# Two halves of the tokens set apart at every change of stage, and four tiles of each FFN with tokens as rows

## Chip, cores and metric

The kernel runs on 1 core of one Trainium2 chip. The metric is the device time of one execution in microseconds (us), as the median of the runs. Computing is in float32, each product of matrices as three products of a high and a low part.

## What is computed

The reference takes x (256 tokens x 1024), and runs three blocks of layers over it. Two belong to the first model, one to the second. Each FFN is a SwiGLU of 1024 to 2 x 2816 and back, and there are six:

```python
x = x + FFN_RESIDUAL * rmsnorm(swiglu(rmsnorm(x, g[0]), ffn_w_in[i, 0], ffn_w_out[i, 0]), g[1])
h = rmsnorm(x, g[2])
...
x = x + rmsnorm(m, g[3])
x = x + FFN_RESIDUAL * rmsnorm(swiglu(rmsnorm(x, g[4]), ffn_w_in[i, 1], ffn_w_out[i, 1]), g[5])
gate = jax.nn.sigmoid(rmsnorm(x, g[6]) @ ple_w_gate[i])
x = x + rmsnorm(gate * (p[i] @ ple_w_proj[i]), g[7])
```

Here m is differential attention in the first block, and a state space layer (S5) with a gated linear unit (glu1, glu2) in the second. The third block has no norm behind an FFN; its middle is a sliding window attention and an HGRN2 recurrence side by side (the mixers), joined through `w_out`, and its gate is the last product before the final norm.

## The kernel before, in words

**Weights.** They come in 264 units of 1 MB, in the order of use, by DMAs on the SP queue into `raw` (4 buffers of a unit). A unit is two half units of 128 x 1024. For each half unit ScalarE (ACT) rounds raw to `whi` (line 600) and VectorE (DVE) makes `wlo` = raw - whi (L1060), into one of 4 slots. `use` asks for splits up to 3 half units ahead of the one in hand (`Ahead`, which goes no further than the slots that are free). A slot is free when TensorE (PE) has counted the half unit in `s_used`; a raw buffer when both of its halves have their wlo (`weights` in `sync`).

**Two forms of a product.** An up of an FFN (`half_unit`) holds weights stationary: 8 k-tiles x 3 products, 24 matmuls of 256 columns for one half unit, all 256 tokens at once, result with features as rows. `linear` and the downs hold tokens stationary (`run`): for each token half (128 tokens) and each half unit (a k-tile), 3 x 2 matmuls of 512 columns, so 12 for both halves, result with tokens as rows in four banks of PSUM. All matmuls of both have line 1740.

**An FFN.** 22 tiles of 128 features. Each tile is two ups (gate and value) and one down. Behind an up come silu on ACT (L682), the product on DVE (L1181), its high part on ACT (L686), its low part `hlo` on DVE (L1183). Pairs of tiles alternate with the downs of the pair before; the downs of the last two tiles are one `run`, half 0 before half 1.

**A change of stage.** The result y of token half h goes through these steps (`settle`, `take_turns`):

1. ACT: squares of y, each half row (L630, L633; L627 behind a gate); DVE: y x g (L1115, L1117; L1110).
2. POOL: rstd in two instructions (L490, L497); DVE: added to X (L1137).
3. ACT: squares of X (L643); POOL: rstd.
4. DVE: norm to `xn` (L1145).
5. PE: 8 transposes (L1811); ACT: high part `xhi` (L660).
6. DVE: low part `xlo` (L1165).

`ORDER` says in which turn the two halves take a step, the same on all engines. Each engine works strictly in its program's order.

```python
ORDER = (0, 0, 0, 1, 0, 1, 1, 0, 1, 0, 1, 1)
ORDER_DEFER = (0, 0, 0, 1, 0, 1, 0, 1, 0, 1)
```

With the second (`DEFER`: ahead of v of the attention, and of the gates) half 1's step 5 stands behind the second k-tile of the next `linear`. At the gates (`ple`), `proj` runs within the change of stage, ACT copies its result (L714), then come the gate's sigmoid (L718) and the product with it (L1100), each over a whole row of 1024. While the FFNs, the attention and the mixers run, `Weave` puts one step of the other work (heads, tables, recurrence) between half units at each `fill`.

## Time and profile before

| | us |
|---|---|
| median of 3 runs | 1938.12 |
| lowest, highest | 1934.77, 1940.52 |
| the profiled execution, its own time | 1937.2 |
| its span (first to last instruction) | 1935.4 |
| TensorE busy in it | 1739.7 |
| VectorE, ScalarE, GpSimd busy | 1113.4, 887.7, 132.5 |
| mean granted TensorE clock | 0.921 |
| moved by DMA | 300.95 MB, 155 GB/s |

How to read it: the profile is of one execution. A row of the timeline gives start and length, the engine, the line of the kernel, the operation with what it writes and reads, and in brackets how long the engine stood idle before it and who released it. The length of a matmul is more than its share of the engine, since matmuls overlap: the pitch is read from a piece of the chain or from two starts. The clock is 1.00 at 2.4 GHz and 0.50 at 1.2 GHz.

### The profile page before, as it was taken

The page shows a single profiled execution, that of the slowest core. Times are in us where ns is not written, and L with a number is a line of the kernel's source. Part 1 is how long each engine was busy: PE and PEld are TensorE (multiplying, and loading weights), DVE is VectorE, ACT ScalarE, POOL GpSimd, SP SyncE. Part 2 cuts the span into 40 slices and gives each one's busy share as a digit, 9 for nine tenths or more (in the row PEclk, how much of TensorE's full clock was granted, in tenths as well). Part 3 has the DMA queues.
Part 4 walks back from the last instruction along what each step waited for, and adds up shares of the span by engine and source line. Part 5 has one row for each costly group of instructions (what it writes and reads, how often), then busy time and mean ns, then how long its engine had stood idle before and what let it go on. Part 6 is the DMA issues. An engine that isn't in the chain of part 4 may idle for free.

```text
span 1935.4 us, 27710 instructions
## 1 busy us (share of the span) xinstructions
PE 1739.7 (90%) x11666; PEld 1601.0 (83%) x11666; DVE 1113.4 (58%) x1587; ACT 887.7 (46%) x1365; POOL 132.5 (7%) x197
## 2 busy tenths in 40 slices
PE   7999897699987999978488999889998997999996
PEld 7999795699976998967468999679998886899995
DVE  5555565475555744649455555555555675655554
ACT  5444554344444536430444444544445434444443
POOL 0000000100002012840000000000000000000000
PEclk9999997799998979966588999989999998999998
DMA  7654442255544533520054555445454431445550
GB/s 282 236 195 175 176 156 80 86 201 185 194 174 144 193 119 133 184 77 1 22 195 152 180 183 187 174 155 206 176 195 148 150 108 66 173 169 176 195 189 28
DMA packets 51083, 300.95 MB, mean 155 GB/s; under 512 B 6072, under 2 KB 12688, under 8 KB 17168
## 3 DMA queue, kind: packets, MB, share of 16 engines
q1 hardware_dynamic: 50800, 298.66, 43.2%
q8 instruction: 92, 1.51, 0.3%
q0 software_dynamic: 160, 0.52, 0.1%
q14 instruction: 31, 0.25, 0.0%
HBM read 298.08 MB, written 1.09 MB: 155 GB/s over the span
## 4 chain that ended last, share of the span: by engine, by line
PE 79%; DVE 9%; ACT 7%; issue 2%; POOL 2%; DMA 0%; DVEq 0%; SPq 0%; ACTq 0%; POOLq 0%
PE PS L1740 75%; DVE wlo L1060 1%; ACT wk L643 1%; PE PS L1743 1%; ACT whi L600 1%; POOL st L497 1%; PE PS L1811 1%; DVE wk L1435 1%; DVE SC L1307 1%; DVE wk L1437 1%; DVE X L1137 1%; DVE wk L1439 1%; DVE xn L1145 1%; ACT SC L820 1%; ACT SC L855 1%
## 5 line engine op out<-in xcount | busy, mean ns | idle before, releaser
L1060 DVE TENSOR_TENSOR wlo<-raw,whi 128x1024 fp32r<-128x1024 f32 x528 | 651.2, 1238 | 418.9 <-ACT whi L600 418.1
L1740 PE MATMUL PS<-xhi,whi 128*128 128x256 f32 x2536 | 730.8, 288 | 11.5 <-DVE xlo L1165 8.5
L1740 PE MATMUL PS<-xlo,whi 128*128 128x256 f32 x2536 | 725.3, 286 | 0.0
L1740 PE MATMUL PS<-xhi,wlo 128*128 128x256 f32 x2536 | 724.7, 286 | 0.0
L600 ACT ACTIVATE whi<-raw 128x1024 fp32r<-128x1024 f32 x528 | 551.8, 1054 | 368.5 <-PE PS L1740 368.4
L1740 PEld LDWEIGHTS PS<-xhi,whi 128*128 128x128 f32 x2536 | 494.5, 195 | 20.3 <-DVE xlo L1165 10.9
L1740 PEld LDWEIGHTS PS<-xlo,whi 128*128 128x128 f32 x2536 | 494.8, 195 | 2.1
L1740 PEld LDWEIGHTS PS<-xhi,wlo 128*128 128x128 f32 x2536 | 494.2, 195 | 0.0
L1740 PE MATMUL PS<-whi,hhi 128*128 128x512 f32 x544 | 169.9, 394 | 0.2 <-issue 0.2
L1740 PE MATMUL PS<-wlo,hhi 128*128 128x512 f32 x544 | 168.8, 391 | 0.0
L1740 PE MATMUL PS<-whi,hlo 128*128 128x512 f32 x544 | 168.2, 390 | 0.0
L682 ACT ACTIVATE wk<-PS 128x256 f32<-128x256 f32 x132 | 50.5, 383 | 217.6 <-PE PS L1740 217.4
L1181 DVE TENSOR_TENSOR wk<-PS,wk 128x256 f32<-128x256 f32 x132 | 55.9, 424 | 119.4 <-ACT wk L682 119.4
L1740 PEld LDWEIGHTS PS<-wlo,hhi 128*128 128x128 f32 x544 | 102.7, 189 | 22.2
L1740 PEld LDWEIGHTS PS<-whi,hlo 128*128 128x128 f32 x544 | 102.6, 189 | 21.9
L1740 PEld LDWEIGHTS PS<-whi,hhi 128*128 128x128 f32 x544 | 98.5, 190 | 17.3 <-issue 0.6
L1740 PE MATMUL PS<-whi,xhi 128*128 128x512 f32 (+1 forms) x256 | 87.3, 414 | 21.9 <-ACT SC L714 11.8
L686 ACT ACTIVATE hhi<-wk 128x256 fp32r<-128x256 f32 x132 | 55.2, 418 | 91.8 <-DVE wk L1181 91.8
L1811 PE MATMUL PS<-idt,xn 128*128 128x128 f32 x176 | 35.9, 366 | 67.8 <-DVE xn L1145 67.8
L1183 DVE TENSOR_TENSOR hlo<-wk,hhi 128x256 fp32r<-128x256 f32 x132 | 57.3, 434 | 64.0 <-ACT hhi L686 64.0
L1811 PEld LDWEIGHTS PS<-idt,xn 128*128 128x128 f32 x176 | 28.4, 189 | 75.9 <-DVE xn L1145 60.2
L490 POOL TENSOR_SCALAR st<-st 128x1 f32<-128x1 f32 x36 | 11.7, 325 | 1151.2 <-ACT wk L633 599.8
(252 smaller groups left out, 1539.3 us busy)
## 6 DMA issues: line engine op xcount, KB each, us to landing
raw<-in_w SPq DMA_DIRECT2D x264, 1024.0 KB, 4.8
gr<-in_rows SPq DMA_DIRECT2D x23, 512.0 KB, 3.8
SC<-scratch SPq DMA_DIRECT2D x1, 2048.0 KB, 8.1
SC<-scratch SPq DMA_DIRECT2D x2, 1024.0 KB, 8.5
X<-in_x SPq DMA_DIRECT2D x2, 512.0 KB, 4.4
xn<-in_sc SPq DMA_DIRECT2D x2, 512.0 KB, 7.0
out<-xn SPq DMA_DIRECT2D x2, 512.0 KB, 2.6
SC<-in_pT SPq DMA_DIRECT2D x3, 256.0 KB, 4.2
```

Source lines behind the costliest of these rows:

```text
L497: g.tensor_tensor(r, ms, mh[:, 0:max(n, 1)], ALU.pow).then_inc(done, 1)
L600: a.activation(whi[:, u % NSPLIT, :], raw[:, u // 2 % NRAW, u % 2 * HU:u % 2 * HU + HU], ACT.Copy).then_inc(s_hi, 1)
L643: a.activation(wk[:, f], X[:, h, f], ACT.Square, scale=1 / 32, accum_out=ss[:, i:i + 1]).then_inc(s_sq, 1)
L682: a.activation(sg[:, f % 2, :], PS[:, b, 0:S], ACT.Silu).then_inc(s_silu, 1)
L686: a.activation(hhi[:, f % 4, :], hf[:, f % 2, :], ACT.Copy).then_inc(s_hhi, 1)
L820: e = a.activation(cst[r, k, :, s, 16 * i:16 * i + 16], o[k][r], ACT.Copy)
L855: e = a.activation(o[32 * j:32 * j + 32, :, :, v], p[32 * v:32 * v + 32, :, j, :], ACT.Gelu_apprx_tanh)
L1060: v.tensor_tensor(wlo[:, u % NSPLIT, :], src, hi.bitcast(f32), SUB).then_inc(s_lo, 1)
L1181: v.tensor_tensor(hf[:, f % 2, :], PS[:, 4 + f % 3, S:2 * S], sg[:, f % 2, :], MUL).then_inc(s_hm, 1)
L1183: v.tensor_tensor(hlo[:, f % 4, :], hf[:, f % 2, :], hhi[:, f % 4, :].bitcast(f32), SUB).then_inc(s_hlo, 1)
L1740: return pe.matmul(o, l, r, start=start, stop=stop)
L1811: e = pe.transpose(PS[:, tr_bank(k, h, kq), 128 * i:128 * i + 128], xn[:, h, 128 * (4 * kq + i):128 * (4 * kq + i) + 128], idt[:, :])
```

## The change

- **Slots.** `raw` has 2 buffers, not 4, and `whi` and `wlo` have 6 slots, not 4. The splits no longer look at which slots are free: each place in the programs of ACT and DVE names the half unit up to which it splits (`split`).
- **Order at a change of stage.** `settle(k, h, mid, end)` does all steps of half 0, then all of half 1. Between norm and the low part stands a split up to `mid`, behind it one up to `end`.
- **PE** begins the next product with half 0: k-tiles 0 to 5, then half 1's 0 and 1, half 0's 6 and 7, half 1's 2 to 7 (`halves`); half 1's transposes stand within (behind k-tile 4 of half 0 in an FFN and 3 in v; at a gate behind 2, with the next stage's transposes of half 0 ahead of the last part).
- **FFN.** The ups of tiles 0 to 3 (8 half units) have tokens stationary, like `linear`; silu and product are in place with tokens as rows, then 4 transposes for each half, then the high and low parts. Tiles 4 and 5 each stand alone with the downs of 0 to 3 between. The tail has four tiles (`TAIL`), not two; so has `wo`, and `w_out` and `glu2` have six.
- **Gates** read `proj` from PSUM; sigmoid, product and g are done by half rows. glu2's bias has a buffer of its own. The mixers' product `ri` comes first there, half by half, where it stood between the first pairs and the rest; `fill(4)` becomes `fill(5)`.

```diff
-NRAW = 4
-NSPLIT = 4
+NRAW = 2
+NSLOT = 6
 AHEAD = 3
+NA = 4
+NW = NF - NA
+TAIL = 4
...
 def up_at(n, f):
-    return FFN_AT[n] + (2 * f if f < 2 else 4 + 6 * (f // 2 - 1) + 2 * (f % 2))
+    return FFN_AT[n] + (8, 12)[f - NA] if f < NA + 2 else FFN_AT[n] + 16 + 6 * (f // 2 - 3) + 2 * (f % 2)
 def down_at(n, f):
-    j = f // 2
-    return FFN_AT[n] + (8 + 6 * j if j < NF // 2 - 1 else 64) + f % 2
+    if f < NA:
+        return FFN_AT[n] + 10 + 4 * (f // 2) + f % 2
+    return FFN_AT[n] + (20 + 6 * (f // 2 - 2) if f < NF - 2 else 64) + f % 2
...
-        while self.n <= min(v + AHEAD, N_HALF - 1) and (self.n < NSPLIT or self.n - NSPLIT <= self.done):
+        while self.n <= min(v, N_HALF - 1):
...
-                while at[0] <= min((v + AHEAD - 1) // 2 + NRAW, N_HALF // 2 - 1):
+                while at[0] <= min((v - 1) // 2 + NRAW, N_HALF // 2 - 1):
...
-                weights(LAST[BEFORE[k]] - 1 if k else -9)
+                weights(LAST[BEFORE[k]] + 4 if k else 3)
...
+            def settle(k, h, mid=-1, end=-1):
+                times_g(k, h)
+                add_x(k, h)
+                norm(k, h)
+                split(mid)
+                evict_lo(k, h)
+                split(end)
...
             def ffn(n):
+                u0 = FFN_AT[n]
+                split(u0 + 7)
+                for h in range(2):
+                    q.wait_ge(e_silu, 2 * n + h + 1)
+                    if h:
+                        q.wait_ge(e_tr, 2 * n + 1)
+                    v.tensor_tensor(wk[:, HI], PS[:, 5 + 2 * h, :], wk[:, LO], MUL).then_inc(e_hm, 1)
+                    split(u0 + (9, 13)[h])
+                    q.wait_ge(e_hhi, 2 * n + h + 1)
+                    t = slice(128 * h, 128 * h + 128)
+                    v.tensor_tensor(hlo[:, 0:4, t], in128(PS[:, 4 + 2 * h, :]), hhi[:, 0:4, t].bitcast(f32), SUB).then_inc(e_hlo, 1)
+                    if h == 0:
...
                 k = (3, 7, 11)[layer]
-                def rest():
-                    evict_lo(k, 1)
-                take_turns(k, steps, {3: lambda: linear(f"proj{layer}", 2, head=2, tail=0)})
-                linear(f"gate{layer}", 8, head=4, tail=2, finish=rest)
-                take_turns(k + 1, steps)
+                u = PLE_AT[layer]
+                settle(k, 0, u + 2, u + 3)
+                settle(k, 1, u + 5, u + 9)
+                for h in range(2):
+                    settle(k + 1, h, *((u + 11, u + 13), (u + 15, u + 15))[h])
...
+            def run(parts, base, last, by_half=None, between={}, order=None):
+                for h, n in order or [(h, n) for h in range(2) for n in range(len(parts))]:
+                    if by_half is not None and n == 0:
                         q.wait_ge(s_xlo, n_ev(by_half, h))
-                    for n, (u, ahi, alo, first, end) in enumerate(parts):
-                        if finish and h == 0 and n == 2:
-                            finish()
-                        hi, lo = weight(u)
-                        l_hi, l_lo = ahi[:, 128 * h:128 * h + 128], alo[:, 128 * h:128 * h + 128]
-                        for i, (l, r) in enumerate(((l_hi, hi), (l_hi, lo), (l_lo, hi))):
-                            for c in range(2):
-                                e = mm(PS[:, base + 2 * h + c, :], l, r[:, 512 * c:512 * c + 512], first and i == 0, end and i == 2)
-                        if h:
-                            e.then_inc(s_used, 1)
-                        elif last and n == len(parts) - 1:
-                            e.then_inc(s_y, 1)
...
+                            at[0, n] = lambda k=k: ready(k)
...
+            def halves(*spans):
+                return [(h, n) for h, a, b in spans for n in range(a, b)]
...
                 k = (0, 2, 4, 6, 8, 10)[n]
-                def up(f):
+                def turned_half(h):
+                    b = 4 + 2 * h
+                    q.wait_ge(e_hm, 2 * n + h + 1)
+                    for i in range(4):
+                        e = pe.transpose(PS[:, b, 128 * i:128 * i + 128], wk[:, 512 + 128 * i:640 + 128 * i], idt[:, :])
+                    e.then_inc(e_tr, 1)
+                def up(f, between=None):
                     b = 4 + f % 3
-                    if f >= 3:
-                        q.wait_ge(s_hm, NF * n + f - 2)
-                    if f == 0:
-                        q.wait_ge(s_xlo, n_ev(k, 1))
-                    half_unit(up_at(n, f), PS[:, b, 0:S])
-                    bg.fill()
-                    half_unit(up_at(n, f) + 1, PS[:, b, S:2 * S])
-                    bg.fill()
+                    if f >= NA + 3:
+                        q.wait_ge(s_hm, nth(n, f) - 2)
+                    for i in range(2):
+                        half_unit(up_at(n, f) + i, PS[:, b, S * i:S * i + S])
+                        if between and i == 0:
+                            between()
+                        bg.fill()
                 def part(f):
-                    q.wait_ge(s_hlo, NF * n + f + 1)
+                    if f < NA:
+                        q.wait_ge(e_hlo, 2 * n + 2)
+                    else:
+                        q.wait_ge(s_hlo, nth(n, f) + 1)
                     return down_at(n, f), hhi[:, f % 4, :], hlo[:, f % 4, :], f == 0, f == NF - 1
-                for j in range(NF // 2):
+                def down(f):
+                    weight(down_at(n, f))
+                    run([part(f)], 0, False)
+                    bg.fill(2)
+                def other_half():
+                    transposed(k, 1)
+                    if k in GATED:
+                        q.wait_ge(s_gated, n_gate(k, 1))
+                    if k == 2:
+                        q.wait_ge(s_yg, n_yg(k, 1))
+                        q.wait_ge(s_sq, n_sq(k, 1, 1))
+                if first:
+                    transposed(k, 0)
+                linear(f"first{n}", x_acts, 4, by_half=k, between={(0, 5 if k else 2): other_half, (1, 6): lambda: turned_half(0)},
+                       order=halves((0, 0, 6), (1, 0, 2), (0, 6, 8), (1, 2, 8)), n_fill=0)
+                for f in range(NA, NA + 2):
+                    up(f, (lambda: turned_half(1)) if f == NA else None)
+                    down(2 * (f - NA))
+                    down(2 * (f - NA) + 1)
+                for j in range(3, NF // 2):
                     up(2 * j)
                     up(2 * j + 1)
-                    for f in (2 * j - 2, 2 * j - 1) if j else ():
-                        weight(down_at(n, f))
-                        run([part(f)], 0, False)
-                        bg.fill(2)
-                run([part(NF - 2), part(NF - 1)], 0, True)
+                    if 2 * j < NF - TAIL + 2:
+                        down(2 * j - 2)
+                        down(2 * j - 1)
+                run([part(f) for f in range(NF - TAIL, NF)], 0, True)
             def ple(layer):
                 k = (3, 7, 11)[layer]
-                def project():
-                    q.wait_ge(s_plo, layer + 1)
-                    linear(f"proj{layer}", p_acts, 4, head=2, tail=0)
-                settle(k, {3: project})
-                q.wait_ge(s_prj, 2 * layer + 2)
-                linear(f"gate{layer}", x_acts, 4, head=4, tail=2, by_half=k, finish=lambda: transposed(k, 1))
-                settle(k + 1)
+                q.wait_ge(s_plo, layer + 1)
+                q.wait_ge(s_hm, nth((1, 3, 5)[layer], NF))
+                v0 = PLE_AT[layer]
+                parts = [(v0 + i, *p_acts[i], i == 0, i == 1) for i in range(2)]
+                run(parts, 4, True, None, {(1, 0): lambda: transposed(k, 0)})
+                at = {(0, 3): lambda: transposed(k, 1)}
+                if layer < 2:
+                    at[1, 7] = lambda: transposed(k + 1, 0)
+                linear(f"gate{layer}", x_acts, 0, by_half=k, between=at, order=halves((0, 0, 4), (1, 0, 2), (0, 4, 8), (1, 2, 8)))
...
-                linear("v", x_acts, 0, head=4, by_half=1, finish=lambda: transposed(1, 1))
+                transposed(1, 0)
+                linear("v", x_acts, 0, by_half=1, between={(0, 4): lambda: transposed(1, 1)},
+                       order=halves((0, 0, 6), (1, 0, 2), (0, 6, 8), (1, 2, 8)))
...
-                q.wait_ge(s_xlo, n_ev(9, 1))
+                transposed(9, 0)
+                for h in range(2):
+                    q.wait_ge(s_xlo, n_ev(9, h))
+                    for c in range(4):
+                        hi, lo = weight(u0[0] + c)
...
+        rows_(np.concatenate([w_in[:, 0:128 * NA], w_in[:, FF:FF + 128 * NA]], 1))
+        for j in range(2):
+            up(NA + j)
+            rows_(down[j])
+        for j in range(3, NF // 2):
+            up(2 * j)
+            up(2 * j + 1)
+            rows_(down[j - 1])
```

**Order of DVE** from `wo` to FFN 1, from the first step of half 0 on. Before:

```order
L1115 TENSOR_TENSOR xn<-PS,gr 128x512 [waits s_y,s_row1]
L1117 TENSOR_TENSOR xn<-PS,gr 128x512 [waits s_sq]
L1137 SCALAR_TENSOR_TENSOR X<-xn,st,X 128x512 [waits s_yg,s_r1,s_X]
L1137 SCALAR_TENSOR_TENSOR X<-xn,st,X 128x512
L1115 TENSOR_TENSOR xn<-PS,gr 128x512 [waits s_used]
L1117 TENSOR_TENSOR xn<-PS,gr 128x512 [waits s_sq]
L1145 SCALAR_TENSOR_TENSOR xn<-X,st,gr 128x512 [waits s_r2,s_row0]
L1145 SCALAR_TENSOR_TENSOR xn<-X,st,gr 128x512
L1137 SCALAR_TENSOR_TENSOR X<-xn,st,X 128x512 [waits s_yg,s_r1,s_X]
L1137 SCALAR_TENSOR_TENSOR X<-xn,st,X 128x512
L1145 SCALAR_TENSOR_TENSOR xn<-X,st,gr 128x512 [waits s_r2]
L1145 SCALAR_TENSOR_TENSOR xn<-X,st,gr 128x512
```

and now (L1064 is the split, L1123 and L1125 y x g, L1145 the sum, L1153 norm, L1173 the low part):

```order
L1123 TENSOR_TENSOR xn<-PS,gr 128x512 [waits s_y,s_row1]
L1125 TENSOR_TENSOR xn<-PS,gr 128x512 [waits s_sq]
L1145 SCALAR_TENSOR_TENSOR X<-xn,st,X 128x512 [waits s_yg,s_r1,s_X]
L1145 SCALAR_TENSOR_TENSOR X<-xn,st,X 128x512
L1153 SCALAR_TENSOR_TENSOR xn<-X,st,gr 128x512 [waits s_r2,s_row0]
L1153 SCALAR_TENSOR_TENSOR xn<-X,st,gr 128x512
L1064 TENSOR_TENSOR wlo<-raw,whi 128x1024 [waits s_hi] x3
L1173 TENSOR_TENSOR xlo<-PS,xhi 128x4x128 [waits s_xhi] x2
L1064 TENSOR_TENSOR wlo<-raw,whi 128x1024 [waits s_hi]
L1123 TENSOR_TENSOR xn<-PS,gr 128x512 [waits s_used]
L1125 TENSOR_TENSOR xn<-PS,gr 128x512 [waits s_sq]
L1145 SCALAR_TENSOR_TENSOR X<-xn,st,X 128x512 [waits s_yg,s_r1,s_X]
```

The halves no longer take turns, and three splits stand between norm and the low part of half 0, one more ahead of half 1.

**Order of PE** at the end of an FFN (FFN 0). Before, the last three parts (a single down, then the first of the tail):

```order
L1740 MATMUL PS<-whi,hhi 128x512
L1740 MATMUL PS<-wlo,hhi 128x512 x2
L1740 MATMUL PS<-whi,hlo 128x512 x2
L1740 MATMUL PS<-whi,hhi 128x512 x2
L1740 MATMUL PS<-wlo,hhi 128x512 x2
L1740 MATMUL PS<-whi,hlo 128x512 x2
L1740 MATMUL PS<-whi,hhi 128x512 [waits s_lo,s_hlo]
L1740 MATMUL PS<-whi,hhi 128x512
L1740 MATMUL PS<-wlo,hhi 128x512 x2
```

and now, from the last matmuls of the last up on:

```order
L1783 MATMUL PS<-xlo,whi 128x256
L1783 MATMUL PS<-xhi,wlo 128x256
L1783 MATMUL PS<-whi,hhi 128x512 [waits s_hlo,s_lo]
L1783 MATMUL PS<-whi,hhi 128x512
L1783 MATMUL PS<-wlo,hhi 128x512 x2
L1783 MATMUL PS<-whi,hlo 128x512 x2
L1783 MATMUL PS<-whi,hhi 128x512 [waits s_lo]
L1783 MATMUL PS<-whi,hhi 128x512
L1783 MATMUL PS<-wlo,hhi 128x512 x2
```

The wait for the low part of the last tile stood behind the downs of two tiles; now it stands right behind the last up.

**Order of PE** in the first product of FFN 1 now, from the end of k-tile 4 of half 0 (L1860 are transposes):

```order
L1783 MATMUL PS<-whi,xlo 128x512 x2
L1860 MATMUL PS<-idt,xn 128x128 [waits s_xn]
L1860 MATMUL PS<-idt,xn 128x128 x3
L1860 MATMUL PS<-idt,xn 128x128 [waits s_xn]
L1860 MATMUL PS<-idt,xn 128x128 x3
L1783 MATMUL PS<-whi,xhi 128x512 [waits s_lo,s_sq,s_yg]
L1783 MATMUL PS<-whi,xhi 128x512
L1783 MATMUL PS<-wlo,xhi 128x512 x2
L1783 MATMUL PS<-whi,xlo 128x512 x2
L1783 MATMUL PS<-whi,xhi 128x512 [waits s_xlo]
```

Half 1's transposes stand between k-tiles 4 and 5 of half 0; before, PE began no product of an FFN ahead of them.

## Rows read from the trace of the kernel before

**Rows 1.** Page, busy time of each engine.
```profile
PE 1739.7 (90%) x11666; PEld 1601.0 (83%) x11666; DVE 1113.4 (58%) x1587; ACT 887.7 (46%) x1365; POOL 132.5 (7%) x197
```

**Rows 2.** Chain of waits, pieces with nothing to wait for: start, length, what.
```profile
217.84 0.87 PE PS L1811 x8
...
368.90 186.42 PE PS L1740 x1308
...
743.32 2.88 PE PS L1740 x24
...
757.80 2.75 PE PS L1740 x12
```

**Rows 3.** Waits of PE: engine, place, releaser: us, times, longest.
```profile
PE PS L1811 <- DVE xn L1145: 67.8, 17, 9.8
...
PE PS L1740 <- DVE wlo L1060: 10.1, 2, 7.1
```

**Rows 4.** Timeline, wo to FFN 1: start, length, engine, line, operation, idle before.
```profile
353.13 0.60 ACT L630 ACTIVATE wk<-PS 128x512 f32<-128x512 f32 x1 [6.12 <-PE PS L1740]
...
354.70 0.29 POOL L490 TENSOR_SCALAR st<-st 128x1 f32<-128x1 f32 x1 [9.49 <-ACT wk L633]
...
355.73 1.41 DVE L1137 SCALAR_TENSOR_TENSOR X<-xn,st,X 128x512 f32<-128x512 f32 x2 [1.19 <-POOL st L497]
...
359.41 1.41 DVE L1145 SCALAR_TENSOR_TENSOR xn<-X,st,gr 128x512 f32<-128x512 f32 x2
...
360.21 1.97 PE L1811 MATMUL PS<-idt,xn 128*128 128x128 f32 x8 [4.30 <-DVE xn L1145]
...
367.52 0.60 ACT L660 ACTIVATE xhi<-PS 128x512 fp32r<-128x512 f32 x1 [0.26 <-PE PS L1811]
...
368.15 0.69 DVE L1165 TENSOR_TENSOR xlo<-PS,xhi 128x512 fp32r<-128x512 f32 x1 [0.16 <-ACT xhi L660]
...
368.90 0.58 PE L1740 MATMUL PS<-xhi,whi 128*128 128x256 f32 x1 [1.41 <-DVE xlo L1165]
```

**Rows 5.** Stretches: length, PE busy (instructions), clock, DMA share, GB/s.
```profile
193.93:237.62 43.69, 37.18 (x162) 0.92 0.48 177
353.05:368.90 15.85, 6.79 (x29) 0.72 0.20 62
546.96:611.05 64.09, 46.59 (x202) 0.85 0.43 162
828.18:857.24 29.06, 14.98 (x67) 0.73 0.27 101
1007.30:1027.92 20.62, 6.64 (x28) 0.61 0.39 124
1448.91:1469.60 20.69, 14.26 (x66) 0.91 0.45 169
1685.90:1698.24 12.34, 6.00 (x29) 0.86 0.38 127
1875.61:1935.40 59.79, 43.07 (x186) 0.87 0.18 67
611.05:616.00 4.95, 4.95 (x23) 0.50 0.25 64
```

**Rows 6.** Timeline behind the last matmul of an up, FFN 0.
```profile
176.95 0.63 PE L1740 MATMUL PS<-whi,hhi 128*128 128x512 f32 x2
...
178.47 0.43 DVE L1183 TENSOR_TENSOR hlo<-wk,hhi 128x256 fp32r<-128x256 f32 x1 [0.48 <-ACT hhi L686]
```

**Rows 7.** Timeline, four splits in a row on ACT and DVE.
```profile
13.30 3.88 ACT L600 ACTIVATE whi<-raw 128x1024 fp32r<-128x1024 f32 x4
...
14.38 4.63 DVE L1060 TENSOR_TENSOR wlo<-raw,whi 128x1024 fp32r<-128x1024 f32 x4 [0.25 <-ACT whi L600]
```

**Rows 8.** Tile raw on the SP queue, all 264 loads.
```profile
DMA to landing us min/median/max: 4.6/4.8/14.4
```

**Rows 9.** Stretch of the mixers: PE, PEld, DVE, ACT, POOL busy, clock.
```profile
1469.60:1640.84 171.24, 157.40 (x1463) 144.25 (x1463) 108.43 (x182) 79.62 (x141) 1.85 (x2) 0.96 0.34 118
```

More of the change, by code:

```diff
@@ L795, in attention @@
                     bg.fill()
[L796 removed]
+                linear("wo", 8, tail=4, there=lambda k: bg.drain() if k == 6 else None, n_fill=2)
             def turns_():
@@ L1035, in scalar @@
             bg.drain()
-            settle(5)
+            squares(PLACED, 0)
+            squares2(PLACED, 0)
+            squares(PLACED, 1)
+            squares2(PLACED, 1)
+            for h in range(2):
+                evict_hi(PLACED, h)
             s5()
@@ L1718, in vector @@
             bg.drain()
-            take_turns(5, steps)
+            for h in range(2):
+                times_g(PLACED, h)
+                add_x(PLACED, h)
+                norm(PLACED, h)
+            for h in range(2):
+                place_u(PLACED, h)
             s5()
@@ L1746, in weight @@
                 q.wait_ge(s_lo, u + 1)
-                return whi[:, u % NSPLIT, :], wlo[:, u % NSPLIT, :]
-            def run(parts, base, last, by_half=None, finish=None):
-                for h in range(2):
-                    if by_half is not None:
+                return whi[:, u % NSLOT, :], wlo[:, u % NSLOT, :]
+            def run(parts, base, last, by_half=None, between={}, order=None):
+                for h, n in order or [(h, n) for h in range(2) for n in range(len(parts))]:
+                    if by_half is not None and n == 0:
@@ L1767, in linear @@
-            def linear(name, acts, base=0, head=1, tail=1, by_half=None, finish=None, ready=None, n_fill=1):
+                    if (h, n) in between:
+                        between[h, n]()
+                    u, ahi, alo, first, end = parts[n]
+                    hi, lo = weight(u)
+                    l_hi, l_lo = ahi[:, 128 * h:128 * h + 128], alo[:, 128 * h:128 * h + 128]
+                    for i, (l, r) in enumerate(((l_hi, hi), (l_hi, lo), (l_lo, hi))):
+                        for c in range(2):
+                            e = mm(PS[:, base + 2 * h + c, :], l, r[:, 512 * c:512 * c + 512], first and i == 0, end and i == 2)
@@ L1768, in linear @@
+                    if h:
+                        e.then_inc(s_used, 1)
+                    elif last and n == len(parts) - 1:
+                        e.then_inc(s_y, 1)
+            def linear(name, acts, base=0, head=1, tail=1, by_half=None, between={}, ready=None, n_fill=1, order=None):
                 kts = len(acts)
                 v0 = LAST[name] - kts + 1
-                for ks in groups(kts, head, tail):
+                for ks in [list(range(kts))] if order else groups(kts, head, tail):
+                    at = dict(between) if len(ks) > 1 else {}
@@ L2009, in s5 @@
                 q.wait_ge(s_gelu, 2)
-                linear("glu2", x_acts, 0, tail=2)
-                settle(6)
+                linear("glu2", x_acts, 0, tail=6, between={(1, 5): lambda: transposed(6, 0)})
             def mixers():
```

470 lines of the change are left out of this document (232 added, 238 removed).

## Prediction

> **What bounds the kernel.** I read the page's busy shares first: TensorE 90%, with 195.7 us of its span idle [rows 1]. Nothing else is near: VectorE 58%, ScalarE 46%, so a faster kernel must have less work, or less idle time, on TensorE. Then the pieces of the chain, which give the pitch of its work where nothing waits: a half unit with weights stationary (24 matmuls of 256 columns) takes 2.88 us; 12 matmuls of 512 columns with tokens stationary take 2.75; eight transposes 0.87, at the lower clock 1.98; an FFN runs from its first matmul to the end of token half 0 as one piece of 186.42, so to the end of half 1 189.1 [rows 2]. Inside an FFN there is thus nothing to win but the form of the work. The idle time is at the changes of stage: 67.8 us in 17 waits of the transposes for the normalised tokens [rows 3]. The change at wo to FFN 1 shows why [rows 4]: from the end of `wo`'s half 0 (353.05) to the first FFN matmul (368.90) are 15.85 us, of which half 1's last two parts cover 2.7. The chain is squares, rstd on POOL, add to X, squares, rstd, norm, transpose, evict, once per half, nearly all of it in turn, and TensorE needs both halves. The row by stretch gives every such place whole, with its clock [rows 5].
>
> **The form of the first four tiles.** Eight half units per FFN go from 2.88 to 2.75: 8 x 0.13 x 6 = 6.2 us less. Their product must then be transposed, 8 transposes of 0.11 per FFN: 0.9 x 6 = 5.4 more. Net under 1 us: the form only lets half 0 run alone. The Trainium skill (TensorE: Matmul & The Clock Gate, Back-to-back issue gap) gives columns / 2.4 GHz + 2.5 ns, 109 and 216 ns for the two widths; the rows give 120 and 229 ns, so by the rule the form would be worth 8 x 0.03 x 6 = 1.4 us, the net would be a loss of 4.0, and the end of my sum 4.8 us later. The rows are this kernel's own instructions, so the rule gets no chance of its own; the sum goes by the rows.
>
> **A new wait at each FFN's end.** Before, the downs of tiles 18 and 19 ran between the last up and the tail. Now the tail is four tiles, and its list of parts waits for the split of tile 21 before its first matmul (the order of PE, shown above). From an up's last matmul to its hlo are silu, product, hi, lo: next matmul at 176.95, hlo ready at 178.90 [rows 6]. That is 2.0 us idle, 6 times: +12 us, inside the figures below.
>
> **A change of stage, worked out: wo to FFN 1.** t = 0 is the end of `wo`'s half 0. Durations [rows 4]: squares 1.57 to the start of rstd, 1.03 to X, from X through squares and rstd to norm 3.68, of which I take off 0.3 for half 1's product that stood ahead of norm on DVE, norm 1.4, an eviction 0.60 on ACT and 0.69 on DVE; a split 0.97 on ACT and 1.16 on DVE [rows 7].
> - Half 0: norm from 6.1 to 7.5. DVE then has three splits (order of DVE, above): 11.0. Two xlo: 12.35. First matmul at 12.4, not 15.85: 3.4 gained. ACT's three hi are ready in time.
> - Half 1: DVE reaches it only after one more split, 13.5. Its y has been ready since 5.5. g twice, squares, rstd, X, squares, rstd: norm from 19.5 to 20.9, split of k-tile 4 to 22.1.
> - TensorE: k-tiles 0 to 3 of half 0 from 12.4 to 19.4 (3.3 us of it at the lower clock, as after the change before, where the first 5 us ran at 0.50 [rows 5]; 1.6 lost). Idle 2.8 for k-tile 4's split. That part and the transposes of half 1 end at 24.4. K-tile 5's split stands behind half 1's evictions: 0.6, 1.4, 1.0 (ACT) and 1.2: idle 3.2. K-tile 6 needs the slot that half 1's first part frees: 1.0 + 1.2 + 0.3 of hand-over less the 1.37 of the next part: idle 1.1.
> - Sum to the end of FFN 1: 12.4 + 186.6 (the FFN at full pitch, new form and transposes in) + 0.9 (half 1's transposes, now inside) + 7.1 idle + 1.6 clock = 208.6. Before: 15.85 + 189.1 = 205.0. So +3.6. Up to 2.7 comes back, since two parts of half 1 moved behind the drain of the heads; I take +2.3.
>
> So running ahead gains the start and gives it back in waits for weights, because splits and both halves' chains stand in one order on DVE and ACT.
>
> **The other places by the same addition**, each with its 2.0 where an FFN ends ahead of it, from last up (or end of half 0, made equal in work) to the end of the stage behind [rows 5]:
> - Start to end of FFN 0: first matmul at 12.9 where it was 15.76, then waits of 1 to 2 us: -0.4.
> - FFN 0 to q/k of the attention: 43.7 to 45.9: +2.2.
> - FFN 1 to gate to the end of FFN 2: 64.1 + 189.1 = 253.2 to 251.9. Idle for a k-tile behind half 1's norm is 6.4 in the gate and 6.3 in the FFN, but the transposes no longer run at the lower clock with nothing else to do, and sigmoid, gate and product in halves shorten the chain: -1.3. FFN 3 to FFN 4 the same: -1.3.
> - FFN 2 to the state space part: both placements of u (3.6 each on DVE) now stand behind both norms: 29.1 to 29.6: +0.5.
> - glu2 to the end of FFN 3: 20.6 + 189.1 = 209.7 to 207.6, with one idle of 8.3 for k-tile 4: -2.1.
> - FFN 4 to the mixer's pairs: 20.7 + 10.9 (ri, later before) = 31.6 to 29.8: -1.8.
> - w_out to the end of FFN 5: 12.3 + 189.1 = 201.4 to 199.2: -2.2.
> - FFN 5 to the end: 59.8 to 57.7: half 0's last chain runs beside half 1's gate, and half 1's own, in halves, takes 7.0 from the end of the gate to the end of norm: -2.1.
>
> Sum: -0.4 + 2.2 + 2.3 - 1.3 - 1.3 + 0.5 - 2.1 - 1.8 - 2.2 - 2.1 = -6.2 us. The profiled execution took 1937.2 us (span 1935.4), the median of the runs is 1938.12, 0.9 above it: 1932.
>
> **Costed at nothing.** Half the raw buffers: a load lands in 4.8 us [rows 8]; a unit is issued when the unit two before it is split, about three half units (8.4 us) before its own split, so 3 us are over there, and split weights are another 5 us ahead of TensorE. Moving ri ahead of the mixer's pairs: it no longer covers steps of the recurrence, whose DVE work then was 108 of 171 us [rows 9]; fills of 5 for 4 keep their number (75 for 73). Bounds: 0, and the whole 10.9 us of ri as new idle; I take 0 since DVE has a third of the stretch free. The second row buffer for glu's bias, SBUF copies of proj that fall away: off TensorE's path.
>
> **Rivals.**
> 1. The waits for weights are not paid: ACT and DVE get ahead where I put them in turn, and each change of stage pays only its first wait. Then the later idle goes: about 6 + 7 + 12 + 9 + 12 + 6 = 52 us over the places: 1880. Against it: the order of DVE shows the split behind norm, and no unit can be split before its place. A part of it, a third, would give 1915.
> 2. Two raw buffers are too few where other transfers share the queue. The slowest raw load took 14.4 us [rows 8]; with loads of 7 us the margin of 3 is gone, and at 9 each load costs about 1 us. It decides from some 20 of the 264 loads over 8 us, near the bias tables, the state space tables and the row loads: +20 us, 1952. For it: SP waits for half 1's norm with only two units out, where it had four. Against: the bulk runs at 4.8.
> 3. The clock. Before, a change of stage had one long idle, then 3 to 5 us at 0.50 [rows 5]; now it has three or four short ones, and each may bring a lower clock that falls on work nothing hides: 1.6 us x 9 places = +14: 1946. My sum has one such stretch per place, mostly under a wait.
> 4. ri as lost filler: 10.9 us at most, 8 likely, 1940.
> 5. The change does not do what it says, half 0 not starting early: the order of PE excludes it.
>
> **How the numbers follow.** A measurement here can tell 0.3% (5.8 us) from no change: faster is under 1932.3, slower over 1943.9. The sum itself, good to some 8 us either way (1924 to 1940): 0.45, a little over half of it faster by the bound. Rival 1, whole or in part, 0.17. Rival 2 0.13, rival 3 0.14, rival 4 0.11. Faster: 0.27 + 0.17 = 0.44. Same: 0.18 + 0.11 = 0.29. Slower: 0.27. The range leaves out the whole of rival 1 and the far end of 2: 1905 to 1956; the sum's own is 1924 to 1940.
>
> **What would show it.** In the changed profile: waits of PE for DVE's wlo, 10.1 us in two before [rows 3], are now the largest group, 40 to 60 us in some 20 waits, with 8 of 3 us or more. A wait of 2.0 us before the first 512-column matmul on hhi at each of the six FFN ends. The waits for norm fall from 67.8 to about 15. Downs inside an FFN keep their pitch and PE's busy time falls little. Wrong if the wlo waits are under 20 us (then rival 1), if DMA raw releases whi for over 20 us (rival 2), or if the mean clock is under 0.90 (rival 3).

## The result, and the profile after

| | before | changed |
| --- | --- | --- |
| median of 4 runs, us | 1938.79 | 1956.68 |
| range, us | 1934.77 to 1940.52 | 1955.04 to 1957.83 |
| profiled execution, span | 1935.4 | 1956.0 |
| TensorE idle in the span | 195.7 | 209.6 |
| mean granted clock | 0.921 | 0.928 |

The ratio is 1.0095, with a 95% interval of 1.0077 to 1.0112: slower by 18 us, where the prediction said 1932 and allowed 1905 to 1956. First the busy line of the changed kernel's page, for [rows 1], and its waits of PE, for [rows 3] (place, releaser: us in total, times, longest).

```profile
span 1956.0 us, 26459 instructions
PE 1746.4 (89%) x11138; PEld 1570.8 (80%) x11138; DVE 1097.5 (56%) x1577; ACT 866.0 (44%) x1355; POOL 123.6 (6%) x197
```

```profile
PE PS L1783 <- DVE wlo L1064: 69.3, 25, 7.4
PE PS L1860 <- DVE xn L1153: 17.5, 7, 7.9
PE PS L1783 <- DVE xlo L1173: 14.1, 10, 3.9
PE PS L1783 <- DVE hlo L1210: 12.4, 6, 2.2
PE PS L1852 <- DVE xn L1153: 12.2, 2, 7.0
...
PE PS L1786 <- DVE SC L1580: 7.6, 4, 2.5
```

The change did what it says. The transposes wait 29.7 us for norms (17.5 + 12.2) where they waited 78.1 (67.8 + 10.3). But weights are now waited for 69.3 us in 25 places, a wait of 12.4 in six places is new, and so is most of the 7.6 in the recurrence (2.7 before). Idle time grew by 14 us, and TensorE's busy time by 6.7, though its first tiles have the cheaper form and only 48 transposes are new: much of its work ran at a lower clock, as shown below.

Against the prediction's terms, by the timeline of PE, from the end of an FFN's last up to the next such end:

| stretch | predicted, us | before, after | measured |
| --- | --- | --- | --- |
| start to FFN 0 | -0.4 | 193.9, 195.2 | +1.3 |
| FFN 0 to FFN 1 | +4.5 | 353.0, 358.5 | +5.4 |
| FFN 1 to FFN 2 | -1.3 | 281.2, 275.8 | -5.4 |
| FFN 2 to the state space part | +0.5 | 29.1, 36.5 | +7.4 |
| from there to FFN 3 | -2.1 | 348.6, 352.9 | +4.2 |
| FFN 3 to FFN 4 | -1.3 | 243.0, 243.9 | +0.8 |
| FFN 4 to the mixers' last transposes | -1.8 | 183.9, 186.0 | +2.1 |
| from there to FFN 5 | -2.2 | 242.8, 247.3 | +4.5 |
| FFN 5 to the end | -2.1 | 59.8, 59.9 | +0.1 |
| sum | -6.2 | 1935.4, 1956.0 | +20.6 |

**The clock.** The tail of FFN 1, from its new wait on, and as a stretch (length, busy of PE, PEld, DVE, ACT, POOL, clock, DMA share, GB/s):

```profile
555.72 0.70 PE L1783 MATMUL PS<-whi,hhi 128*128 128x512 f32 x2 [2.04 <-DVE hlo L1210]
556.26 0.67 PE L1783 MATMUL PS<-wlo,hhi 128*128 128x512 f32 x2
556.73 1.05 PE L1783 MATMUL PS<-whi,hlo 128*128 128x512 f32 x2
557.58 1.05 PE L1783 MATMUL PS<-whi,hhi 128*128 128x512 f32 x2
...
560.13 0.62 PE L1783 MATMUL PS<-whi,hhi 128*128 128x512 f32 x2
560.59 0.62 PE L1783 MATMUL PS<-wlo,hhi 128*128 128x512 f32 x2
```

```profile
555.72:560.13 4.41, 4.41 (x12) 3.48 (x13) 3.59 (x3) 2.24 (x3) 0.00 (x0) 0.61 0.46 130
583.38:586.10 2.72, 2.72 (x6) 2.04 (x7) 1.08 (x1) 0.00 (x0) 0.00 (x0) 0.50 0.69 218
```

A row of two matmuls is followed by the next after 0.46 us at full pitch and after 0.85 in the middle. Twelve matmuls at full pitch are 2.7 us, here they took 4.41: 1.6 lost to the clock and 0.1 to the start, so this wait of 2.04 us costs 3.6. The second stretch is what follows a wait of 5.9 us for a weight: 1.4 lost in its six matmuls and 0.8 more in the eight transposes behind them, which took 1.68 where they take 0.87 at full clock. Summed over the timeline (for each matmul of 256 or 512 columns at the slow pitch, its pitch less the 0.120 or 0.2275 us that it has elsewhere), the loss at the lower clock is 46.0 us before and 57.6 after. Where the line between slow and full pitch is drawn moves each of the two by about 3 us, and their difference lies between 10 and 15. Idle +14 and clock +11.6 are 25.5, which is 5 more than the 20.6 that the time grew by. The cheaper form of the first tiles and fewer transposes at the lower clock go that way; how much each gives was not measured.

**Half 1's chain ahead of a weight.** Timeline of the gate behind FFN 1, up to its k-tile 2, whose weight is the fifth half unit from the projection's first:

```profile
576.07 0.20 ACT L616 ACTIVATION_READ_ACCUMULATOR wk<-PS 128x1 f32 x1
577.39 1.42 DVE L1145 SCALAR_TENSOR_TENSOR X<-xn,st,X 128x512 f32<-128x512 f32 x2 [1.25 <-POOL st L492]
578.18 0.63 ACT L626 ACTIVATE wk<-X 128x512 f32<-128x512 f32 x1 [1.91 <-DVE X L1145]
579.62 1.99 ACT L588 ACTIVATE whi<-raw 128x1024 fp32r<-128x1024 f32 x2
580.77 1.42 DVE L1153 SCALAR_TENSOR_TENSOR xn<-X,st,gr 128x512 f32<-128x512 f32 x2 [1.97 <-POOL st L492]
582.11 2.35 DVE L1064 TENSOR_TENSOR wlo<-raw,whi 128x1024 fp32r<-128x1024 f32 x2
583.38 1.22 PE L1783 MATMUL PS<-whi,xhi 128*128 128x512 f32 x2 [5.87 <-DVE wlo L1064]
```

TensorE wants the weight at 577.5. ACT stands idle for 1.9 us and DVE for 1.3 and 2.0 inside the chain, and the split stands behind both.

**GpSimd's tables, new on the path.** GpSimd and DVE behind FFN 2:

```profile
841.20 2.61 POOL L537 COPY SC<-xn 64x512 f32<-64x512 f32 x4
...
843.95 0.69 DVE L1123 TENSOR_TENSOR xn<-PS,gr 128x512 f32<-128x512 f32 x1 [6.23 <-POOL SC L537]
...
858.65 7.26 DVE L1164 COPY xn<-PS 32x256 f32<-32x256 f32 x16
```

Half 0's y was ready at 839.1, but the product goes to `xn`, from which GpSimd still copies tables. Before, GpSimd was done at 829.0 and VectorE's product began at 836.6, so nothing waited for it. Its work starts at a fill that TensorE runs between the ups, and the first four tiles no longer have fills.

**A load behind a wait.** glu2 in the changed kernel, first SyncE's queue, then ACT and PE:

```profile
998.78 13.05 SPq L390 DMA_DIRECT2D raw<-in_w  x4
```

```profile
1005.56 2.00 ACT L588 ACTIVATE whi<-raw 128x1024 fp32r<-128x1024 f32 x2 [11.43 <-DMA raw<-in_w]
...
1007.93 1.22 PE L1783 MATMUL PS<-whi,xhi 128*128 128x512 f32 x2 [2.66 <-DVE wlo L1064]
```

The buffer was free at 989.9. The load was issued at 998.8 because SyncE waited for glu1's two products (done 998.4) to load a row.

### The profile page after: what moved, and what is told of

It is laid out like the page before. It is cut to its first block, busy times and chain, and to the rows that moved or that the text cites. A ratio compares the mean times of both kernels' runs of the same rounds, so it can differ in the third digit from the quotient of the medians.

```text
span 1956.0 us, 26459 instructions
## 1 busy us (share of the span) xinstructions
PE 1746.4 (89%) x11138; PEld 1570.8 (80%) x11138; DVE 1097.5 (56%) x1577; ACT 866.0 (44%) x1355; POOL 123.6 (6%) x197
## 4 chain that ended last, share of the span: by engine, by line
PE 73%; DVE 12%; ACT 7%; POOL 4%; issue 2%; DMA 1%; DVEq 0%; POOLq 0%; ACTq 0%; SPq 0%
PE PS L1783 70%; DVE wlo L1064 3%; ACT whi L588 2%; DVE xn L1153 1%; POOL st L492 1%; ACT wk L626 1%; PE PS L1786 1%; POOL xn L531 1%; DVE wk L1468 1%; PE PS L1860 1%; DVE wk L1470 1%; POOL SC L537 1%; ACT wk L616 1%; DVE X L1145 1%; DVE wk L1472 1%
## 5 line engine op out<-in xcount | busy, mean ns | idle before, releaser
L1064 DVE TENSOR_TENSOR wlo<-raw,whi 128x1024 fp32r<-128x1024 f32 x528 | 640.7, 1236 | 346.4 <-ACT whi L588 342.8
L1783 PE MATMUL PS<-xhi,whi 128*128 128x256 f32 x2152 | 615.6, 286 | 0.0
L1783 PE MATMUL PS<-xlo,whi 128*128 128x256 f32 x2152 | 611.7, 284 | 0.0
L1783 PE MATMUL PS<-xhi,wlo 128*128 128x256 f32 x2152 | 611.6, 284 | 0.0
L1783 PEld LDWEIGHTS PS<-xhi,whi 128*128 128x128 f32 x2152 | 415.8, 193 | 5.4 <-issue 1.5
L1783 PEld LDWEIGHTS PS<-xlo,whi 128*128 128x128 f32 x2152 | 415.6, 193 | 2.4
L1783 PE MATMUL PS<-whi,xhi 128*128 128x512 f32 (+1 forms) x448 | 156.1, 426 | 83.6 <-DVE wlo L1064 69.3
L1783 PE MATMUL PS<-whi,hhi 128*128 128x512 f32 x544 | 174.7, 403 | 12.7 <-DVE hlo L1210 12.4
L1783 PEld LDWEIGHTS PS<-whi,xhi 128*128 128x128 f32 x448 | 86.1, 203 | 113.2 <-DVE wlo L1064 67.7
L1783 PE MATMUL PS<-wlo,xhi 128*128 128x512 f32 (+1 forms) x448 | 148.3, 408 | 0.0
L1783 PE MATMUL PS<-whi,xlo 128*128 128x512 f32 (+1 forms) x448 | 147.8, 407 | 0.0
L1783 PEld LDWEIGHTS PS<-wlo,xhi 128*128 128x128 f32 x448 | 90.4, 202 | 20.1
L1783 PEld LDWEIGHTS PS<-whi,xlo 128*128 128x128 f32 x448 | 90.1, 201 | 19.9
```

The costliest lines, as they stand in the source:

```text
L1064: v.tensor_tensor(wlo[:, i, :], src, whi[:, i, :].bitcast(f32), SUB).then_inc(s_lo, 1)
L1783: return pe.matmul(o, l, r, start=start, stop=stop)
```

## Experiments

All were timed beside the kernel before. Those of different sets are compared by their ratio to it; the changed kernel's is 1.0095 (1.0077 to 1.0112). In the table, idle is TensorE's in the span, and the last column the loss at the lower clock as above. Both are from one execution of each kernel, and where the clock falls differs from one to the next, so a difference of a few us in the last column alone says little.

| kernel | median | ratio, 95% interval | idle | clock |
| --- | --- | --- | --- | --- |
| before_tail_wait | 1954.4 | 1.0084, 1.0070 to 1.0098 | 203.1 | 50.5 |
| before_short_wait | 1949.8 | 1.0058, 1.0046 to 1.0071 | 204.2 | 48.3 |
| lazy_tail | 1942.1 | 1.0021, 1.0011 to 1.0030 | 202.4 | 47.7 |
| gap_splits | 1925.1 | 0.9926, 0.9912 to 0.9939 | 183.8 | 48.7 |
| gaps_half1 | 1926.1 | 0.9926, 0.9913 to 0.9940 | 190.5 | 53.1 |
| tables_fill | 1959.9 | 1.0112, 1.0099 to 1.0126 | 207.8 | 58.0 |
| ri_back | 1954.8 | 1.0081, 1.0068 to 1.0093 | 210.2 | 53.7 |
| glu_load | 1953.0 | 1.0077, 1.0065 to 1.0090 | 208.2 | 56.0 |
| phi_late | 1959.4 | 1.0109, 1.0095 to 1.0123 | 210.3 | 57.4 |
| lazy_gaps | 1919.4 | 0.9904, 0.9888 to 0.9919 | 180.2 | 47.7 |
| lazy_gaps_phi | 1911.3 | 0.9859, 0.9845 to 0.9872 | 175.8 | 46.6 |
| lazy_gaps_phi_t2 | 1913.8 | 0.9873, 0.9859 to 0.9886 | 175.7 | not read |
| all_four | 1913.4 | 0.9861, 0.9846 to 0.9876 | 175.0 | 46.2 |

**before_tail_wait: the new wait put into the kernel before.**

```diff
                     for f in (2 * j - 2, 2 * j - 1) if j else ():
+                        if f == NF - 4:
+                            q.wait_ge(s_hlo, NF * n + NF)
                         weight(down_at(n, f))
```

> The kernel before with the changed kernel's wait alone: in each of the six FFNs TensorE waits for the split of tile 21 ahead of the down of tile 18. Theory 'idle and clock': each wait is 2.0 us of idle and then 1.4 to 1.6 us more, since in the changed kernel's trace the matmuls of the next 3.4 us take about twice their time; 6 x 3.5 = 21 us, so 1938.8 + 21 = 1960. Rival 'idle only', the price in the prediction: 6 x 2.0 = 12, so 1951. Rival 'given back' (the next change of stage waits for the same split, so less later): within 3 us of 1939.

It costs 16.3 us, between the two theories. Six waits of 1.84 us are 11.0, but idle time as a whole rises by 7.4, so 3.6 comes back in smaller waits elsewhere (those for norms stay, at 68.1). TensorE's busy time rises by 8.7: 4.5 by the last column, about 1.6 in transposes at the lower clock, and the rest not placed.

**before_short_wait: the same, on `s_hhi`.**

> The kernel before with a shorter dose: ahead of the down of tile 18 TensorE waits for ScalarE's hi of tile 21, which ends about 0.46 us ahead of its split, so six waits of some 1.4 us instead of 1.84. In the traces waits of 1.1 us are followed by matmuls at full pitch, waits of 2.0 us by about 1.5 us of loss at the lower clock; between the two nothing shows it in full 512-column work. Theory 'the clock falls for waits from some length on, and 1.4 us is still below it': 6 x 1.4 = 8 us, and less what the changes of stage give back: 1944 to 1947. Rival 'nearly as much as the long dose': in proportion, 1.4 / 1.84 of its 16.3 us: 1951.

It costs 11.7, in proportion, as the rival says; so the times show no step. The stretches right behind the waits differ (columns as above; the clock is the third number from the end). Of before_short_wait, FFN 2, after 1.38 us of wait:

```profile
835.04:839.50 4.46, 4.46 (x19) 3.68 (x20) 1.84 (x3) 1.96 (x2) 0.00 (x0) 1.00 0.38 114
```

Of before_tail_wait, FFNs 2 and 1, after 1.84 us each:

```profile
836.18:840.50 4.32, 4.32 (x12) 3.42 (x13) 1.23 (x1) 0.43 (x1) 0.00 (x0) 0.60 0.39 106
554.92:559.30 4.38, 4.38 (x19) 3.65 (x20) 1.40 (x2) 1.50 (x2) 0.00 (x0) 1.00 0.35 110
```

After the short wait the clock stayed at 1.00 in all six FFNs, after 1.84 us it fell in two of six (1.6 lost each time), in the changed kernel's profile after 2.04 to 2.24 in six of six (1.5 to 1.6 each, 9.4 in all). That looks like a step between 1.4 and 2.0 us, but it isn't one. Six of the kernels below keep the same wait of 2.04 to 2.24 us, and in their profiles the clock fell behind 16 of 36: in gap_splits, ri_back and glu_load 2 of 6 each, in tables_fill and gaps_half1 3, in phi_late 4. With the changed kernel that is 22 of 42. At the end of FFN 3 in glu_load, and of FFN 4 in gap_splits:

```profile
1217.63 0.70 PE L1783 MATMUL PS<-whi,hhi 128*128 128x512 f32 x2 [2.04 <-DVE hlo L1210]
1218.17 0.62 PE L1783 MATMUL PS<-wlo,hhi 128*128 128x512 f32 x2
1218.64 0.63 PE L1783 MATMUL PS<-whi,hlo 128*128 128x512 f32 x2
1219.10 0.62 PE L1783 MATMUL PS<-whi,hhi 128*128 128x512 f32 x2
```

```profile
1436.05:1440.50 4.45, 4.45 (x20) 3.67 (x21) 3.57 (x3) 2.24 (x3) 0.00 (x0) 1.00 0.45 133
```

So one of these waits costs 2.0 us or 3.6, about as often the one as the other, and six of six in the changed kernel's profile is in part chance. What decides it was not found. The profiled execution of the short dose is 12.6 us longer than the kernel's before, 4.3 more than its waits of 8.3, without one drop right behind them. From one last up to the next the stretches grow by 0.8 less to 1.3 more than the wait, so the surplus lies in no one place; its cause is open.

**lazy_tail: the waits taken out of the changed kernel.** Each part of the tail waits for its own tile's split.

```diff
-                run([part(f) for f in range(NF - TAIL, NF)], 0, True)
+                run([part(f) for f in range(NF - TAIL, NF)], 0, True,
+                    between={(0, i): lambda i=i: ready(NF - TAIL + i) for i in range(TAIL)})
```

> The changed kernel, but each of the four tail parts waits for its own tile's split just ahead of its first matmul, so the first three find theirs ready. Theory 'idle and clock': all six waits of 2.0 us go and with each about 1.5 us at the lower clock: 1956.7 - 21 = 1936. Rival 'idle only': 1945. Rival 'given back' (half 0 ends earlier but the weights or norms behind it don't): over 1950.

14.6 us come back by the medians (its runs spread over 1937.9 to 1946.8), most of the loss, and between the theory's 21 and the 12 of idle only. The waits of 12.4 us are gone but for 0.6, yet idle fell only 7.2, while the clock gave 9.9; these are from the two profiled executions, which are 18 apart. Of the idle half 5 comes back as other waits, 3.8 of it for GpSimd (its waits of PE; 12.2 before):

```profile
PE PS L1852 <- DVE xn L1153: 16.0, 2, 10.8
```

**gap_splits: the splits moved into the idle time of the chain.** One or two half units per half. In one place, behind `wo`, two more (the first of FFN 1) move ahead of the whole chain.

```diff
-            def settle(k, h, mid=-1, end=-1):
+            def settle(k, h, mid=-1, end=-1, gap=-1):
                 squares(k, h)
+                split(gap)
                 squares2(k, h)
...
                 add_x(k, h)
+                split(gap)
                 norm(k, h)
...
-                settle(k, 1, v + 5, v + 9)
+                settle(k, 1, v + 5, v + 9, v + 5)
```

> The changed kernel, with the splits of one or two half units at each change of stage moved from behind the norm to the idle time inside the chain of the norm (ScalarE: between the two pairs of squares, VectorE: between X and norm), nothing else. Theory 'one order on VectorE and ScalarE': the waits for weights came from splits standing behind the norm though both engines idle 1.9 us inside its chain; waits of TensorE for wlo fall from 69 to 35 us or less, and the time by 15 to 30 with the clock: 1932 to 1942. Rival 'raw buffers' (the splits were waiting for loads, two buffers): waits for wlo stay over 55 us and ScalarE's waits for raw grow: 1950 to 1957. Rival 'norm of half 1 decides': wlo waits fall but waits for xn and xlo grow by as much: over 1950.

31.6 us, more than was expected, and the first version faster than the kernel before (ratio 0.9926). Its timeline at the gate behind FFN 1:

```profile
565.01 1.99 ACT L588 ACTIVATE whi<-raw 128x1024 fp32r<-128x1024 f32 x2
...
566.24 1.41 DVE L1147 SCALAR_TENSOR_TENSOR X<-xn,st,X 128x512 f32<-128x512 f32 x2 [1.25 <-POOL st L492]
...
567.57 2.35 DVE L1066 TENSOR_TENSOR wlo<-raw,whi 128x1024 fp32r<-128x1024 f32 x2
...
568.84 1.22 PE L1787 MATMUL PS<-whi,xhi 128*128 128x512 f32 x2 [2.46 <-DVE wlo L1066]
```

The wait of 5.87 is 2.46. The waits for `wlo` fall from 69.3 to 44.5, not to the 35 that the theory gave; those of the transposes rise by 6. Idle as a whole falls by 26 and the clock's loss by 9. Against the rival of the raw buffers: the waits for `wlo` don't stay over 55, and ScalarE's waits for raw grow only from 223 to 234.

**gaps_half1: half 1's splits alone.**

> The changed kernel with the splits moved inside the norm chain for token half 1 alone; half 0 keeps its three splits behind the norm. If half 1's waits for k-tile 4 (5.9, 5.8, 5.9, 5.7 us in the gates and FFNs 2 and 4, 7.4 in FFN 3) are the cause, most of the 31.6 us gain of both halves stays: 1928 to 1935. If half 0's splits are worth as much (first matmuls earlier by one split of 1.2 us and the half behind it too, nine times): 1938 to 1945.

By the ratio it is all of the gain. Its five runs spread over 1920 to 1935.5 and the profiled one was the slowest, so it is open whether half 0's part is worth nothing or some microseconds.

**tables_fill: the lost fills put back.**

```diff
                 def up(f):
-                    half_unit(up_at(n, f))
-                    half_unit(up_at(n, f) + 1)
+                    for i in range(2):
+                        half_unit(up_at(n, f) + i, 3 if n == 2 and f < NA + 2 else 1)
```

> The changed kernel, with the eight fills of the tables that fell away with the first four tiles of FFN 2 put back at its fifth and sixth (three instead of one behind each half unit, on TensorE, VectorE and ScalarE). Theory 'GpSimd late': its table work starts 18 to 22 us later than before and ends at 843.8, and VectorE's first product of half 0 waits 4.3 us for it; with the fills back that wait goes and with it perhaps 1 us of clock: 1956.7 - 5 = 1952. Rival (the start is not set by the fills, or half 1 alone decides): within 1.5 us of 1956.7.

A miss that teaches. From FFN 2's last up to the state space part it takes 29.9 us instead of 36.5: the two waits for norms fall from 12.2 to 8.3, so GpSimd was a cause there, and 1.6 is the clock, which here did not fall behind the FFN's end. But from FFN 2's first matmul to its last up it takes 229.0 instead of 219.3. In the changed kernel those fills ran behind the last up, under the wait; so its loss of 7.4 there has a gain ahead of it, in the -5.4 of the table. As a whole it is 3 us slower by the medians, with overlapping intervals: no gain is sure, a loss is not.

**ri_back: ri in its old place.**

> The changed kernel with ri back behind the sliding window's heads, where the kernel before has it (both halves together, fills of 4 and 2). Theory 'ri is worth more at the change of stage' (the prediction costed its move at nothing): the recurrence's waits on VectorE (7.6 us in four places against 2.7 before) and about 1.7 us of clock come back, 6 us, but TensorE then waits for both norms behind FFN 4, about 10 us idle and clock: slower than the changed kernel, 1958 to 1964. Rival 4 of the prediction ('ri as lost filler', 8 us likely): faster, 1948 to 1952. In between: the two cancel, 1954 to 1958.

From FFN 4's last up to the mixers' last transposes: 186.2, against 186.0. The recurrence's waits come back, and a wait of 6.9 us for the norm of half 1 stands in their place. As a whole 1954.8, and the interval overlaps with the changed kernel's: what its move costs and what it gains at the change of stage cancel.

**glu_load: one load ahead of the wait on SyncE.**

```diff
-            weights(LAST["glu1"])
+            weights(LAST["glu1"] + 2)
             q.wait_ge(s_z1, 2)
```

> The changed kernel, where the queue of loads issues one more weight unit in front of its wait for the two products of glu1. In the trace of the changed kernel that unit's buffer was free at 989.9, SyncE issued its load at 998.8 behind the wait, it landed at 1005.6, and TensorE waited 2.7 us for its split with 3.0 us at the lower clock behind it. Theory 'two raw buffers behind a wait on the load queue' (rival 2 of the prediction, in this one place): the wait goes, 1956.7 - 5.6 = 1951. Rival (TensorE only waits elsewhere, for half 1's norm in FFN 3): 1955 to 1957.

By the medians 3.7 us, but the intervals overlap, and idle falls by 1.4 alone, since the first wait behind FFN 2 grows by 1.6. So the load behind a wait is shown as the cause of the wait at glu2, and not what mending it is worth. In its trace the wait of 2.66 is 0.96:

```profile
1009.79 0.73 PE L1783 MATMUL PS<-whi,xhi 128*128 128x512 f32 x2 [0.96 <-DVE wlo L1064]
```

**phi_late: the projection's input behind the first tiles.**

> The changed kernel with only the split of the projection's input moved behind the first four tiles. In its trace k-tile 6 is late behind its slot or half 1's evictions rather than behind this load, so less than the 8.1 us that it gave in the other version: 0 to 3 us, 1953 to 1957. Rival (it is paid here as well): 1947 to 1950.

No gain: 1959.4, a little above the 1953 to 1957 that were expected, with an interval that overlaps with the changed kernel's. That the wait for weights has another cause ahead of it is the reading of the trace, and fits.

**lazy_gaps: both large ones.**

> The tail's waits per tile and the splits inside the norm chain, both. If the two are independent: 1956.7 - 14.6 - 31.6 = 1910.5, within 3. If they compete for the same time at a change of stage (half 0 of the norm is ready sooner, weights then late again): 1915 to 1922.

They compete: 5.7 us on top of gap_splits, not 14.6. Behind FFN 2 the first transposes wait 10.8 us again, and behind FFN 0 they wait 3.2, where it was 1.6.

**lazy_gaps_phi.** With the weights sooner, a DMA wait shows. The timeline of FFN 3 in gap_splits:

```profile
1028.47 0.63 ACT L708 ACTIVATE phi<-SC 128x512 fp32r<-128x512 f32 x1 [5.15 <-DMA SC<-in_pT]
1029.01 1.99 ACT L588 ACTIVATE whi<-raw 128x1024 fp32r<-128x1024 f32 x2
...
1031.36 1.22 PE L1787 MATMUL PS<-whi,xhi 128*128 128x512 f32 x2 [4.25 <-DVE wlo L1066]
```

> As lazy_gaps, and the split of the small projection's input (phi, plo) stands behind the first four tiles of FFNs 1, 3 and 5 instead of ahead of their weights. In the trace with splits in the gaps, ScalarE waits 5.2 and 3.0 us there for the load of pT with two weight splits queued behind it, and TensorE 4.3 and 1.9 us for those. Theory 'a DMA wait ahead of splits': 6 us of waits go, and with them up to 3 us of clock: 5 to 8 us faster than lazy_gaps. Rival (the split of k-tile 6 is late anyway for its slot): within 2 us of it.

8.1 us, by an edit that did nothing alone. It is the fastest version: 1911.3 us, ratio 0.9859. The busy line of its page:

```profile
span 1910.6 us, 26471 instructions
PE 1734.8 (91%) x11138; PEld 1561.2 (82%) x11138; DVE 1096.9 (57%) x1577; ACT 866.1 (45%) x1355; POOL 129.9 (7%) x197
```

**lazy_gaps_phi_t2 and all_four.**

> As lazy_gaps_phi, with half of the extra fills for the tables in FFN 2 (two behind each half unit of its fifth and sixth tile). With the tail's waits gone TensorE ends FFN 2 sooner and waits the longer for GpSimd's tables (10.8 us for the first norm). Theory 'GpSimd's chain ends last': its start moves up by about 5 us at about as much TensorE work that then lies in FFN 2 instead of in the wait: 0 to 4 faster than lazy_gaps_phi. Rival 'the fills only move': 0 to 3 slower, as with all eight.

> The fastest version so far (tail's waits per tile, splits inside the norm chain, projection's input later: 1911.3) with the earlier load at glu2 as well. If that is worth the same here: 1906. If the change of stage behind it takes it back: 1910 to 1912.

Neither adds anything: 1913.8 and 1913.4, with intervals that overlap with 1911.3's. The earlier load at glu2 is taken back in FFN 3, where k-tile 4 then waits 4.6 us instead of 3.8.

## Why the prediction was wrong

- **What bounds the kernel: right.** Nothing is won inside an FFN, and a change of stage gains its start and gives it back in waits for weights. The idle time of the worked place held: its first matmul, 12.4 us behind the end of `wo`'s half 0, came at 12.4; k-tiles 4, 5 and 6 of FFN 1 at 2.8, 3.2 and 1.1 us were 2.1, 3.0 and 1.1; gate and FFN 2 at 6.4 and 6.3 were 5.9 and 5.8; FFN 3's 8.3 was 7.4. In all, the waits for weights were put at 40 to 60 us in some 20 places and were 69.3 in 25; those for norms at about 15, and were 17.5 (without the 12.2 behind FFN 2).
- **"My sum has one such stretch per place": the step that failed, and the largest term, 11.6 us.** A change of stage now has two to four waits, and in the changed kernel's profile most that are 2 us or longer bring the clock down. In the worked place the sum had 1.6 us for the clock; behind the first matmul and the waits for k-tiles 4 and 5 it was about 4.5, which is nearly all by which that place, up to its FFN's end, came out longer. That was rival 3, at 14 per cent. Its sign was badly chosen: the mean granted clock rose from 0.921 to 0.928, since it counts idle stretches too. The loss must be read from the pitch of the matmuls: 57.6 for 46.0.
- **"A new wait at each FFN's end": the same step.** The size of the wait was right (12.4 for 12), its price was not. "That is 2.0 us idle, 6 times: +12 us" left out what follows at the lower clock: 9.4 us in the profiled execution, about half as much in the average of the seven profiles with this wait. Taking it out gives 14.6 (lazy_tail), putting a slightly shorter one into the kernel before costs 16.3.
- **FFN 2 to the state space part, +0.5: missed a wait.** I followed half 0 and half 1 over DVE, ACT and POOL, but took the tables on GpSimd as done, as before. It cost 4.3 us, part of the +7.4. The fills that the first tiles lose were in the diff. That the stretch ahead came out 4 better than the sum fits with the same fills, but was not shown apart.
- **The tails of six parts (glu2, w_out): not in the sum.** Loads and splits for six parts come one behind the other, 2.7 us of idle at glu2, 1.3 + 2.8 at w_out, and 3.0 at the lower clock at glu2. Two raw buffers were "costed at nothing"; here that was wrong (rival 2, in two of 25 waits: 2.7 at glu2 and 2.8 at w_out, each behind a split that ScalarE could only begin when a load had landed). Its test too was wrong: loads release ACT for 223 us of the trace, nearly all of it while TensorE has its weights.
- **ri costed at nothing: wrong as a term.** The recurrence waits 4.9 us more. That ri_back is no slower or faster says only that its new place gains about as much at the change of stage, which the sum had counted beside it.
- **The rest** (FFN 5 to the end, -2.1 predicted, +0.1 measured): 2.0 of wait and 1.6 of clock at FFN 5's end, of which the sum held the first.

Against the profiled execution the sum was wrong by 27 us. Named above are 11.6 for the clock (about 9 of it at the FFNs' ends), 4.3 for GpSimd, 6.8 of idle for the six-part tails and 4.9 for the recurrence, less 4 in the stretch up to FFN 2's end, put down to the tables' fills: 24. The rest is not placed, and the share of the clock is the least sure: it is one execution's, and known to some 3 us. Three raw buffers beside six slots were not run, so the price of the halved loads as a whole stays open.

## What to carry to other kernels

Price a new wait on TensorE by its length and by what may follow it at the lower clock: here waits of 1.84 and 2.04 us cost 2.7 and 2.4 us each in the time (16.3 put in, 14.6 taken out, six waits each). Look at more than one profile before calling it a rule when the clock falls. Where an engine's program is one fixed order, put work that another engine needs soon into the idle time inside a dependency chain, not behind it: that alone turned a loss of 18 us into a gain of 14 (0.9926). When work is moved earlier, ask of each background task that used its places (here the fills for GpSimd's tables) who waits for its end.
